# First norm of an encoder block: POOL sums the squares of eight tiles into one, TensorE sums that one tile

## The reference

```
x = x + 1/2 * SwiGLU_1(RMSNorm(x))
h = RMSNorm(x);  projections of h -> retention + windowed attention -> gated merge
x = x + W_out(merge)
x = x + 1/2 * SwiGLU_2(RMSNorm(x))
y = RMSNorm(x)
```

## Time and profile before

| | |
|---|---|
| median of 3 runs | 2127.97 us (2126.57 to 2141.17) |
| the profiled execution | 2131.22 us |
| its span, first to last instruction | 2129.4 us |
| PE busy | 2055.8 us, 97% of the span |
| DVE busy | 1290.2 us, 61% |
| ACT busy | 733.4 us, 34% |
| POOL busy | 931.8 us, 44% |
| TensorE clock granted, mean | 0.989 of full |

### The profile page before, as it was taken

How to read it: one execution, slowest core, us unless ns; L and a number is a source line. 1 busy time by engine, 2 the same in 40 slices (tenths; PEclk the granted TensorE clock), 3 DMA queues, 4 the chain that set the end, 5 groups by cost and what they waited for, 6 DMA issues and landing times. The chain is left out here.

```text
span 2129.4 us, 26163 instructions
## 1 busy us (share of the span) xinstructions
PE 2055.8 (97%) x9240; PEld 1670.0 (78%) x9240; DVE 1290.2 (61%) x1439; ACT 733.4 (34%) x973; POOL 931.8 (44%) x588
## 2 busy tenths in 40 slices
PE   7999999989989999999999999999999999989997
PEld 6788888867877888888876768888788888867776
DVE  6766666677766343543755555467666666677653
ACT  5433333343334321211134444324333333343331
POOL 0343443469797221221211112252434434477893
PEclk9999999999999999999999999999999999999997
DMA  3232323473433111112211114331323223465331
GB/s 132 95 114 98 113 93 100 138 257 133 156 121 128 60 60 50 49 59 69 70 40 40 49 46 161 136 139 62 126 97 116 90 99 112 162 219 175 132 94 79
DMA packets 105967, 227.25 MB, mean 107 GB/s; under 512 B 9264, under 2 KB 30384, under 8 KB 105904
## 3 DMA queue, kind: packets, MB, share of 16 engines
q1 hardware_dynamic: 74528, 175.14, 24.1%
q10 hardware_dynamic: 31376, 51.29, 6.9%
HBM read 165.05 MB, written 61.34 MB: 106 GB/s over the span
## 5 line engine op out<-in xcount | busy, mean ns | idle before, releaser
L1909 POOL TENSOR_TENSOR w_lo<-stage,w_hi 128x1024 fp32r<-128x1024 f32 x54 | 142.9, 2646 | 439.5 <-ACT w_hi L948 439.5
L1550 DVE SCALAR_TENSOR_TENSOR x<-ps,x 128x512 f32<-128x512 f32 x280 | 190.5, 687 | 140.7 <-PE ps L620 139.4
L558 PE MATMUL ps<-a_hi,w_hi 128*128 128x512 f32 x752 | 254.1, 405 | 3.1 <-DVE q_t L1686 1.9
L558 PE MATMUL ps<-a_lo,w_hi 128*128 128x512 f32 x752 | 243.5, 391 | 0.0
L558 PE MATMUL ps<-a_hi,w_lo 128*128 128x512 f32 x752 | 243.4, 391 | 0.0
L1924 POOL TENSOR_TENSOR gb<-gb,rstd 128x512 f32<-128x512 f32 x42 | 90.0, 2144 | 304.6 <-DVE gb L1474 283.9
L558 PEld LDWEIGHTS ps<-a_hi,w_hi 128*128 128x128 f32 x752 | 140.7, 189 | 32.8 <-issue 2.8
L558 PEld LDWEIGHTS ps<-a_hi,w_lo 128*128 128x128 f32 x752 | 142.0, 189 | 30.1
L558 PEld LDWEIGHTS ps<-a_lo,w_hi 128*128 128x128 f32 x752 | 142.2, 189 | 29.8
L620 PE MATMUL ps<-t_hi,hi 128*128 128x512 f32 x352 | 140.7, 400 | 19.4 <-DVE x L1550 19.4
L620 PE MATMUL ps<-t_hi,hi_a 128*128 128x512 f32 x336 | 132.0, 393 | 6.2 <-ACT tmp L1011 4.6
(11 more groups left out here) (298 smaller groups left out, 4656.7 us busy)
## 6 DMA issues: line engine op xcount, KB each, us to landing
stage<-wstream SPq DMA_DIRECT2D x56, 512.0 KB, 3.3
b_spill<-diff SPq DMA_DIRECT2D x88, 256.0 KB, 3.6
st_a<-win SPq DMA_DIRECT2D x42, 512.0 KB, 3.5
st_b<-win SPq DMA_DIRECT2D x42, 512.0 KB, 4.0
t_lo<-b_spill SPq DMA_DIRECT2D x40, 512.0 KB, 7.8
b_spill<-rawv SPq DMA_DIRECT2D x66, 256.0 KB, 4.1
a_lo<-b_spill SPq DMA_DIRECT2D x30, 512.0 KB, 6.0
x<-xT SPq DMA_DIRECT2D x16, 512.0 KB, 6.6
```

What stands on the lines that cost most here:

```text
L558: mm = pe.matmul(ps[:, bank, :], w[0:r, k, :], mv[0:r, k, HALF * half:HALF * half + HALF], start=first and part == 0, stop=final and part ...
L1550: dve.scalar_tensor_tensor(out=x[:, m, part], in0=ps[:, bank, :], scalar=0.5, in1=x[:, m, part], op0=ALU.mult, op1=ALU.add).then_inc(xacc, 1)
L1909: pool.tensor_tensor(w_lo[:, parity, :, :], stage[:, parity, :, :], f32(w_hi[:, parity, :, :]), ALU.subtract).then_inc(wlo_done, 1)
```

## The change

The squares are no longer summed by PE tile by tile. POOL adds square 0 and square 1 into `rstd`, then adds squares 2 to 7 to it, one by one, each as soon as ACT has written it. `first_sums` and its four calls are gone; behind product r = 2 PE sums the one tile in `rstd` with eight one-column products (`sums(0, 5)`). DVE's `total` of the first norm is gone, since PSUM then holds the eight numbers. ACT waits for POOL's count in place of PE's before it writes T3 and T4 over the squares, and reads the root's input from PSUM. The counters of later norms are renumbered.

```diff
-ACC_AT = (0, 0, KT - 2, 2 * KT - 2)
+ACC_AT = (0, KT - 1, 2 * KT - 3, 3 * KT - 3)
...
             def sums(p, bank):
-                pe.wait_ge(acc_done, ACC_AT[p] + KT)
+                pe.wait_ge(acc_done, ACC_AT[p] + (KT - 1 if p == 0 else KT))
                 column_sums(bank, 0, of_rstd).then_inc(sums_done, 1)
...
-            def first_sums(k):
-                for t in (2 * k, 2 * k + 1):
-                    pe.wait_ge(sq_done, t + 1)
-                    column_sums(5, CH * t, of_square(sq1[t])).then_inc(sq_summed, 1)
...
-                    if k < K4 - 1:
-                        first_sums(k)
...
                 if f == 0:
-                    first_sums(K4 - 1)
+                    sums(0, 5)
...
-                    act.wait_ge(sq_summed, 6)
+                    act.wait_ge(acc_done, 5)
                     act.wait_ge(comb1, 4)
                     high1(2)
                     t_high(f, T3, 16)
...
                 if f == 0:
-                    act.wait_ge(sq_summed, KT)
+                    act.wait_ge(acc_done, KT - 1)
                 t_high(f, T4, 20)
                 if f == 0:
-                    act.wait_ge(total_done, 1)
-                    root(rinv[:, :])
+                    act.wait_ge(sums_done, 1)
+                    root(ps[:, 5, 0:CH])
...
-                    dve.wait_ge(sq_summed, KT)
-                    total(5, KT)
...
+            pool.wait_ge(sq_done, 2)
+            pool.tensor_tensor(two(rstd[:, :]), sq1[0], sq1[1], ALU.add).then_inc(acc_done, 1)
+            for t in range(2, KT):
+                pool.wait_ge(sq_done, t + 1)
+                pool.wait_ge(acc_done, t - 1)
+                pool.tensor_tensor(two(rstd[:, :]), two(rstd[:, :]), sq1[t], ALU.add).then_inc(acc_done, 1)
```

More of the change, by code:

```diff
@@ L264, in block_program @@
         comb2, hi2_done, lo2_done, prod2, xacc = sem("comb2"), sem("hi2_done"), sem("lo2_done"), sem("prod2"), sem("xacc")
-        acc_zero, sq_done, acc_done, sq_summed = sem("acc_zero"), sem("sq_done"), sem("acc_done"), sem("sq_summed")
+        acc_zero, sq_done, acc_done = sem("acc_zero"), sem("sq_done"), sem("acc_done")
         total_done, neg_done = sem("total_done"), sem("neg_done")
@@ L1170, in ffn @@
                     act.wait_ge(wlo_done, U_TAIL2 + 1)
-                    act.wait_ge(sums_done, 2)
+                    act.wait_ge(sums_done, 3)
                     root(ps[:, 5, 0:CH])
@@ L1231, in _ @@
             load_rope(0)
-            act.wait_ge(total_done, 2)
+            act.wait_ge(total_done, 1)
             root(rinv[:, :])
@@ L1380, in _ @@
             ffn(1)
-            act.wait_ge(total_done, 3)
+            act.wait_ge(total_done, 2)
             root(rinv[:, :])
@@ L1692, in scaled @@
                 dve.tensor_tensor(out, slot(bank), rstd[:, :], ALU.mult).then_inc(evac, 1)
-            dve.wait_ge(sums_done, 1)
+            dve.wait_ge(sums_done, 2)
             total(4, 3)
@@ L1893, in _ @@
             ffn(1)
-            dve.wait_ge(sums_done, 3)
+            dve.wait_ge(sums_done, 4)
             total(6, 3)
```

## The result

| | before | changed |
|---|---|---|
| median | 2129.84 us (4 runs, 2126.57 to 2141.17) | 2144.99 us (4 runs, 2142.55 to 2148.39) |
| ratio, 95% interval | | 1.0051, 1.0031 to 1.0072 |
| profiled execution, span | 2131.22, 2129.4 us | 2142.55, 2140.8 us |

The change makes the kernel slower by 0.5%: 10.9 us by the ratio, 6.6 to 15.3 by its interval. The difference of the two medians is 15.2, but the four runs of before spread from 2126.57 to 2141.17. So the ratio is the better number, and 15.2 is probably too much.

The account below looks back on a forecast made before the run. Up to r = 2 the path was taken to be DVE's chain, then ACT's, with PE's earlier sums beside it. DVE's +13.9 and -1.3 at r = 2 and r = 3 gave +12.6 on 2128.0: 2140.6 us, range 2135 to 2147.

Parts of the forecast that it names:

- DVE stands still for each addition: DVE's chain at 12 to 35 us: POOL's seven additions block it, about 2.1 us each, ending it 13.9 us later.
- The bound in which the scaling let an addition pass: Low end for DVE's chain: one addition passes unharmed beside a scaling, five are counted, 1.3 + 10.3 = 11.6 us.
- They take turns, instruction by instruction: DVE and POOL exclude each other per instruction; a turn costs 3.38 us with long DVE operations, 2.83 with half-sized ones.
- Rival C: DVE keeps its turn after POOL's first addition; the others wait until DVE runs dry at 36.8; 2134 us, chance 0.04.
- rival B: Not slower: DVE is held up by less than 1.3 us in all; 2126.7, down to 2124.7 us, chance 0.07.
- Gain at r = 2: PE's sums behind r = 2, on the path: eight products in place of 16, 3.48 to 1.74 us, gain 1.74 us.
- The clock: From r = 2's start to r = 3's end: 9.4 us after low clock following idle PE, against 10.73 before.
- The sum: Whole kernel: +13.9 - 1.3 = +12.6 us, giving 2140.6 us against the median, 0.6% slower.
- PE loses the sums behind steps 0, 1, 2: PE's first steps: 10.5 us of work removed, worth nothing by itself because DVE's chain hides it.
- rival D: PE is the path after all and the sums come off whole, 12.2 us; 2113 to 2116 us, chance 0.02.
- the copy of 42.52: ACT's copy out of PSUM, ending at 42.52 us, for which r = 2 waits at 42.62 behind an idle PE.
- Nothing new behind the spread: After the head: POOL's memset moves with the tail's products, the loop is PE's, and the shift carries to the end.

Follow-up runs that it names:

- the second trace: The kernel before, unchanged, run once more for its trace; span 2132.4 us, T2 at 35.62, r = 2 at 46.37, the spread at 64.39.

## Why the prediction was right, and where it was not

- *DVE stands still for each addition*: shown. Forecast 13.9 us, read 13.74; by instruction, 1.3 forecast and 1.50 read for the first, 2.1 forecast and 1.98 to 2.13 read for the other six. The additions alone reproduce it, three give 5.6, memsets give 1.2 (the scalings), and POOL reading one operand is enough. The bound in which the scaling let an addition pass was wrong: it lost 2.13 us. The prediction's estimate of 2.52 us per addition, from the 2.41 us of an addition and the release time that the Trainium skill, "SBUF — State Buffer", gives, was too high by 0.4 to 0.5. One sign was missed by a little: POOL's additions were to last 2.8 to 3.4 us each, and five of the seven lasted 2.35 to 2.62 (the others 2.95 and 3.16).
- *They take turns, instruction by instruction*: shown by seven additions on seven successive DVE instructions. Rival C, in which DVE keeps its turn, falls with it, and so does rival B, in which it isn't held up. That holding all seven back does not help either was shown by the seven late additions: r = 2 at 56.28.
- *Gain at r = 2*: 1.74 forecast, 1.77 read (3.48 to 1.71).
- *The clock*: 9.4 us forecast from r = 2's start to r = 3's end, 9.81 and 9.38 read in two traces. Nearly all of r = 2 ran at the lower level (0.50 granted) after the 6.46 us of idle time, and r = 3 at the higher one (1.00).
- *The sum*: 12.6 us forecast, 12.82 at the spread against the trace of before that I had. The ratio gives 10.9 (6.6 to 15.3). The prediction held that a measurement tells only about 1% from no change; the interval here is 0.4% wide, so that 0.5% is clear of it. The forecast of the time itself, 2140.6 us, lies 4.4 us under the measured 2145.0; its base, 2128.0, was a median of three runs, and against the larger series of before (2133.80 and 2131.60) the loss is 11.2 and 13.4 us, on either side of 12.6. That the trace agrees to 0.2 us is in part luck: it is compared with the trace of before in which PE was on time, and the two terms of the sum missed by 0.2 (13.9, read 13.74) and 0.4 us (1.3, read 0.92).
- *The step that failed*: "PE loses the sums behind steps 0, 1, 2: 10.5 us, worth nothing by themselves", and with it the grounds against rival D, "the copy of 42.52". Rival D itself, a faster kernel, did not come; its premise, PE as the path, did. The step holds in the first trace, where PE was idle for 0.64 us ahead of r = 2. That was a slack of 0.6 us, and I took one execution for the kernel. In the second trace PE was 3.7 us late there (46.37 against 42.62). Taking the sums away alone won 6 us, 1.1 of which the first trace explains. So part of the change's loss of 12.8 is paid back in those executions of before in which PE is late: against the second trace of before, the change is 7.3 to 7.9 us later at the spread. How often before is in which of the two cases stays open: five traces with these sums, two on time and three late, are too few to say it.
- *Nothing new behind the spread*: no run speaks against it, but the rest of the program varies by 11 us between traces, so a small effect there could not be seen.

## What to carry to other kernels

Before work is given to an idle POOL, look at what DVE does in that stretch: where DVE is the chain that others wait for, each POOL instruction that reads SBUF holds up DVE's two-operand instructions, and with both engines kept busy costs nearly its own length, 2.0 to 2.1 us for an addition of 2.4. Put such work where DVE has slack, and check that no buffer it reads is wanted before then; here the one addition over squares that lie on T4 had such a place, and it paid. And a slack of under 1 us in one trace is not a hidden cost: take a second trace before calling work free.

## What the runs showed of the hardware that I had not expected

- DVE and POOL took strict turns while both had work. Once the second of the seven additions had begun, neither engine ran two instructions in a row until the last was done, whether DVE's instruction was one that takes 0.48 us alone or one that takes 1.24.
- The clock can fall within or behind one-column products though PE's timeline has no gap. In the second trace of before the granted clock was 0.57 to 0.69 over stretches with PE busy to the full; the 12 products of r = 3 took 5.3 us in place of 2.7. In the loop from 60 to 440 us, where the products have 512 columns, it was 1.00 in both traces of before. It does not fall behind every batch: in the first trace the steps that begin at 20.60 and 37.60, right behind such batches, ran at the upper level (0.23 us a product). No run varies the one-column products alone, so this is where the clock fell, not a shown cause.
- A POOL addition of a tile to itself made a turn of 2.3 us with a half-sized DVE instruction, where the addition of two tiles made one of 2.6 to 2.8; a copy took 1.04 us alone, a memset 0.96.
